# One stage of a 256-token block kernel: the two latent norms, the gate scalars and the bank copies behind the direct part are regrouped

## The chip, the core and the metric

One Trainium2 chip, one core. The metric is device microseconds (us) for one execution; lower is better. The kernel before takes 2758.27 us, the median of 3 runs (2757.26 to 2758.77). Its profile is one separate execution.

## The reference

Two transformer blocks run on 256 tokens of width 2048, in float32. The change lies in the first block's input part, which in the reference is:

```python
p = h @ w_in[l]                       # h: normed, modulated x, (256 x 2048)
c_q, c_kv, k_pe, q_g, k_g, v_g, z, b_logit, a_logit, gate_logits = _split_cols(p)
q  = _rmsnorm(c_q, q_norm) @ w_uq     # latents of 512 columns each
kv = _rmsnorm(c_kv, kv_norm) @ w_ukv
qkv = _causal_conv_silu(concat(q_g, k_g, v_g), conv_w)     # 4 taps, then silu
beta = jax.nn.sigmoid(b_logit)
g = -jnp.exp(A_log) * jax.nn.softplus(a_logit + dt_bias)
```

`beta` and `g` feed a chunked gated delta rule over 8 heads, and the normed latents feed 8-head causal attention. Later come the gates, `w_o`, the feed-forward part and the whole second block; the change does not touch those.

## The kernel before, in words

Data lies feature-major: a tile is 128 features by 256 tokens. Weights come from HBM in units of 512 KB, 8 tiles of 128x128 each. For each unit ScalarE rounds it (`hi`, L567, into one of 3 HI buffers) and VectorE subtracts (`lo`, L723, into LO), then TensorE multiplies both parts. A "wide" tile is a 512-column and a 256-column matmul (L361/L362 and L364/L365), a narrow one three of 256 columns (L367 to L369).

The first 16 column blocks of `w_in` are multiplied without that split (the direct part, L389): the 8 latent blocks, the block with `k_pe` and the two logit columns (`BA`), and 7 of the 24 q/k/v blocks. They fill all 8 PSUM banks, two blocks a bank. Their 16 banks' halves are then copied out, and 17 more `w_in` blocks follow as wide tiles, 16 tiles each. The change concerns what runs beside those tiles.

Every engine walks the same Python schedule (`walk`). `do(step, ...)` adds a step to its engine's program and gives a semaphore count to wait for. A side chain is a generator: `later(gen, lag, gap)` starts it `lag` tiles on and lets it make one step whenever `gap` tiles have passed. The list of chains is looked at after every second tile, so a gap of 3 is 4 tiles. `Ring.get` and `need` call `force`, which steps all chains with a gap of up to 3 whatever their due time. Each engine then executes its own program strictly in order. I count tiles from the first wide tile, t = 0.

Per unit, `feed` adds `hi` of a unit three ahead (it waits until TensorE is done with the unit whose buffer it takes) and one unit later its `lo`: `lo` of unit t/8 + 1 stands in VectorE's program at tile t, and TensorE needs it at tile t + 8.

The chains beside the wide tiles:
- `ev_c(j)`: copies latent block j out, squares it (L590), adds squares on GpSimd (`square_add`, L965), and for j = 3 and 7 goes on with `cnorm`: column sum by TensorE (`stat_sum`, L404), root (`root_guess` L603: Ln and Exp; `root_half`, `root_out`), then for each of 4 blocks a scaling (L769), `split_hi` (L578) and `split_lo` (L761) into H2. `finish_steps` of the second half calls `need(H2_tok, 3)`, which forces the chains until the first half is done.
- `ev_kpe`: copies BA and rotates `k_pe` (L422, L805 to L811, L426).
- `scalars`: transposes the logits (L431), `beta` (L613, Sigmoid), `softplus` (L617), then cumulative sums (L436, L437).
- `qkv_chain`: per q/k/v block a first tap on ScalarE (L649), three on VectorE (L817), tanh (L582), product (L769).
- `l2norm(0)`, `l2norm(1)` and `gdn()`, the delta rule, follow.

Of the kernel before, what the change touches and what calls it, by code (L numbers as in the profile page):

```python
# [17 lines left out]
TAPS = (5, 10)  # L18
# [151 lines left out]
def run(gen):  # L170
    for _ in gen:
        pass
# [30 lines left out]
def program(nc, xT, pos, cols_d, consts_d, wada, wst, bias_d, gain_d, out, log):  # L203
# [8 lines left out]
    with ctx:  # L212
# [74 lines left out]
        XSQ = B1[:, 0:16, :]  # L287
        R12, R1, ACC2 = B3[:, 0, :], B3[:, 1, :], B3[:, 2, :]
# [64 lines left out]
        def tensor(e):  # L353
# [190 lines left out]
            walk(dict(tile=tile, tile_tokens=tile_tokens, x_turn=x_turn, direct=direct, c_spread=c_spread, spin=spin, stat_add=stat_add, stat_sum=stat_sum, acc2_sum=acc2_sum, rope_turn=rope_turn, kpe_swap=kpe_swap, ba_turn=ba_turn,  # L544
# [5 lines left out]
        def scalar(e):  # L550
# [131 lines left out]
            def conv_tanh(y, t, ready, free):  # L682
# [4 lines left out]
                      gained=gained, square_sum=square_sum, root_table=root_table, root_guess=root_guess, sine=sine, beta=beta, softplus=softplus, gate_exp=gate_exp, row_square=row_square,  # L687
                      soft_exp=soft_exp, soft_scale=soft_scale, tap_first=tap_first, conv_first=conv_first, padded=padded, turned_rows=turned_rows, turned=turned, g_exp=g_exp, g_copy=g_copy, conv_square=conv_square, conv_affine=conv_affine, conv_tanh=conv_tanh))

        def vector(e):  # L690
# [144 lines left out]
            def cumulated(bk, summed, at):  # L835
# [4 lines left out]
                e.tensor_tensor(DK, GL, GC, sub).then_inc(S["l2_v"], 1)  # L840

# [104 lines left out]
            def conv_silu(t, y, grown):  # L946
# [7 lines left out]
                      ba_copy=ba_copy, softplus_in=softplus_in, decay_log=decay_log, cumulated=cumulated, beta_gate=beta_gate,  # L954
# [32 lines left out]
        def walk(mine, log=None):  # L987
# [386 lines left out]
            SQS = [Stats(x_stat), None]  # L1374

            def ev_c(j):
                def f(bk, tok, own):
                    cq_tok[j] = copy_out(CQ[j], bk, tok, own, x_used)
                    yield
                    while j > 3 and SQS[0].done is None:  # L1380
                        yield
                    if j == 4:
                        SQS[1] = Stats(*SQS[0].before, SQS[0].done)
                    SQS[j // 4].square(CQ[j], cq_tok[j])
                    if j % 4 == 3:
                        yield
                        yield from cnorm(j // 4)
                return f

            H2_tok = [None] * 16  # L1390

            def cnorm(half):
                k = yield from SQS[half].finish_steps(512, 1e-6, *([h_tok[15]] if half == 0 else [need(H2_tok, 3)]))
                name = "q_a_norm" if half == 0 else "kv_a_norm"
                for j in range(4):
                    i, t, fr = tv.get()
# [1185 lines left out]
```

## Time and profile before

| | |
|---|---|
| time, median of 3 runs | 2758.27 us |
| span of the profiled execution, first to last instruction | 2755.3 us |
| time of the profiled execution outside its span | not given on the page |
| TensorE busy | 2684.6 us, 97% |
| VectorE busy | 1931.7 us, 70% |
| ScalarE busy | 1315.8 us, 48% |
| GpSimd busy | 144.1 us, 5% |
| mean granted TensorE clock | 0.996 |

In the profile PE is TensorE, DVE is VectorE, ACT is ScalarE, POOL is GpSimd. Idle time stands in brackets with the instruction that ended it. An instruction's duration can overlap the start of the next; the distance from start to start is what a queue pays.

### The profile page before, as it was taken

Reading aid. Unit: us, or ns where it says so; the run is one execution under the profiler, and the core shown is the slowest. Engines: PE = TensorE matmul, PEld = TensorE weight load, DVE = VectorE, ACT = ScalarE, POOL = GpSimd, SP = SyncE. Lnnn points to the kernel's source line nnn. Section 1 sums busy time; section 2 is a strip of 40 time slices with the busy share of each in tenths; the row PEclk is TensorE's granted clock in tenths of the full one; section 3 lists DMA queues with packets and bytes.
Section 4 is the critical chain, followed back from the end, with each engine's and each line's share of the span. In section 5 each row is a group of like instructions: output and inputs, shape, how many; then the busy total and the mean of one; then the engine's idle time right before and its main releaser. Section 6 shows DMA issues by size and latency. Waiting matters only on the chain.

```text
span 2755.3 us, 41005 instructions
## 1 busy us (share of the span) xinstructions
PE 2684.6 (97%) x16144; PEld 2379.1 (86%) x16144; DVE 1931.7 (70%) x2983; ACT 1315.8 (48%) x2063; POOL 144.1 (5%) x132
## 2 busy tenths in 40 slices
PE   8989999999999999999999999999999999999998
PEld 7768988888899888888888889998888888888887
DVE  6868766876896886655555688997667466575665
ACT  2175644433544544444444454467555444444443
POOL 0000000000002000000000080111100000000000
PEclk9989999999999999999999999999999999999999
DMA  9944346666896786555555555554545555555554
GB/s 386 409 142 154 107 163 219 223 214 219 283 327 239 247 298 213 189 191 188 187 191 190 185 181 177 180 171 138 172 154 190 192 191 191 191 190 193 191 191 146
DMA packets 158737, 565.19 MB, mean 205 GB/s; under 512 B 17616, under 2 KB 21840, under 8 KB 158416
## 3 DMA queue, kind: packets, MB, share of 16 engines
q1 hardware_dynamic: 158544, 562.56, 59.8%
q8 instruction: 128, 2.10, 0.3%
q14 instruction: 65, 0.53, 0.1%
HBM read 560.39 MB, written 2.10 MB: 204 GB/s over the span
## 4 chain that ended last, share of the span: by engine, by line
PE 85%; DVE 8%; ACT 3%; DMA 2%; issue 1%; POOL 0%; DVEq 0%; ACTq 0%; SPq 0%; POOLq 0%
PE BK L364 17%; PE BK L362 17%; PE BK L365 9%; PE BK L361 8%; PE BK L376 4%; PE BK L377 4%; PE BK L378 4%; PE BK L367 4%; PE BK L369 4%; PE BK L368 4%; DVE LO L723 2%; PE BK L389 2%; PE BK L474 2%; DVE B L936 1%; ACT HI L567 1%
## 5 line engine op out<-in xcount | busy, mean ns | idle before, releaser
L567 ACT ACTIVATE HI<-RAW 128x1024 fp32r<-128x1024 f32 x824 | 873.6, 1060 | 1168.5 <-PE BK L362 638.6
L723 DVE TENSOR_TENSOR LO<-RAW,HI 128x1024 fp32r<-128x1024 f32 x824 | 1012.0, 1229 | 381.2 <-ACT HI L567 380.2
L364 PE MATMUL BK<-H,HI 128*128 128x512 f32 x2160 | 869.2, 405 | 17.3 <-DVE LO L723 16.7
L362 PE MATMUL BK<-H,HI 128*128 128x512 f32 x2128 | 840.8, 397 | 0.0
L365 PE MATMUL BK<-H,LO 128*128 128x256 f32 x2160 | 601.5, 278 | 0.0
L361 PE MATMUL BK<-H,LO 128*128 128x256 f32 x2128 | 595.8, 280 | 0.2 <-DVE H L761 0.2
L361 PEld LDWEIGHTS BK<-H,LO 128*128 128x128 f32 x2128 | 401.4, 189 | 93.7 <-DVE H L761 0.6
L365 PEld LDWEIGHTS BK<-H,LO 128*128 128x128 f32 x2160 | 408.2, 189 | 84.9 <-issue 1.0
L364 PEld LDWEIGHTS BK<-H,HI 128*128 128x128 f32 x2160 | 411.5, 190 | 29.7 <-DVE LO L723 20.5
L362 PEld LDWEIGHTS BK<-H,HI 128*128 128x128 f32 x2128 | 400.9, 188 | 3.9
L367 PE MATMUL BK<-H,HI 128*128 128x256 f32 x1280 | 376.2, 294 | 7.9 <-DVE LO L723 6.8
L369 PE MATMUL BK<-H,LO 128*128 128x256 f32 x1280 | 361.9, 283 | 0.0
L368 PE MATMUL BK<-H,HI 128*128 128x256 f32 x1280 | 361.8, 283 | 0.0
L367 PEld LDWEIGHTS BK<-H,HI 128*128 128x128 f32 x1280 | 244.8, 191 | 13.0 <-DVE LO L723 9.6
L368 PEld LDWEIGHTS BK<-H,HI 128*128 128x128 f32 x1280 | 244.9, 191 | 1.5
L369 PEld LDWEIGHTS BK<-H,LO 128*128 128x128 f32 x1280 | 244.6, 191 | 0.0
L376 PE MATMUL BK<-HI,H 128*128 128x512 f32 x512 | 199.2, 389 | 0.0
L378 PE MATMUL BK<-HI,H 128*128 128x512 f32 x512 | 199.2, 389 | 0.0
L377 PE MATMUL BK<-LO,H 128*128 128x512 f32 x512 | 199.2, 389 | 0.0
L761 DVE TENSOR_TENSOR H<-TV,H 128x256 fp32r<-128x256 f32 x116 | 49.2, 425 | 163.7 <-ACT H L578 163.6
L378 PEld LDWEIGHTS BK<-HI,H 128*128 128x128 f32 x512 | 96.1, 188 | 20.2
L377 PEld LDWEIGHTS BK<-LO,H 128*128 128x128 f32 x512 | 96.1, 188 | 19.9
(267 smaller groups left out, 2541.1 us busy)
## 6 DMA issues: line engine op xcount, KB each, us to landing
RAW<-wst_dram SPq DMA_DIRECT2D x837, 512.0 KB, 3.4
RAW<-wada_dram SPq DMA_DIRECT2D x155, 512.0 KB, 4.6
EARLY<-wada_dram SPq DMA_DIRECT2D x37, 512.0 KB, 11.0
EARLY<-wst_dram SPq DMA_DIRECT2D x19, 512.0 KB, 12.2
X<-xT_dram SPq DMA_DIRECT2D x8, 512.0 KB, 7.2
B<-bias_dram SPq DMA_DIRECT2D x32, 128.0 KB, 3.4
out_dram<-B SPq DMA_DIRECT2D x8, 256.0 KB, 2.2
B<-gain_dram SPq DMA_DIRECT2D x1, 1024.0 KB, 4.8
```

Of the source, the lines that this page charges most:

```text
L361: e.matmul(bk[:, 256:512], ll, H[:, k, 0:256], start=False, stop=False, skip_group_check=True)
L362: e.matmul(bk[:, :], hh, H[:, k, :], start=False, stop=last, skip_group_check=True).then_inc(S["tile"], 1)
L364: e.matmul(bk[:, :], hh, H[:, k, :], start=first, stop=False, skip_group_check=True)
L365: e.matmul(bk[:, 256:512], ll, H[:, k, 0:256], start=False, stop=last, skip_group_check=True).then_inc(S["tile"], 1)
L367: e.matmul(bk[:, 0:256], hh, H[:, k, 0:256], start=first, stop=False, skip_group_check=True)
L368: e.matmul(bk[:, 0:256], hh, H[:, k, 256:512], start=False, stop=False, skip_group_check=True)
L369: e.matmul(bk[:, 0:256], ll, H[:, k, 0:256], start=False, stop=last, skip_group_check=True).then_inc(S["tile"], 1)
L376: e.matmul(bks[m][:, :], H[:, k, 128 * m:128 * m + 128], hh, start=first, stop=False, skip_group_check=True)
L377: e.matmul(bks[m][:, :], H[:, k, 128 * m:128 * m + 128], ll, start=False, stop=False, skip_group_check=True)
L378: r = e.matmul(bks[m][:, :], H[:, k, 256 + 128 * m:384 + 128 * m], hh, start=False, stop=last, skip_group_check=True)
L567: e.activation(HI[:, u % NHL, :], raw_at(slot), ACT.Copy).then_inc(S["hi"], 1)
L723: e.tensor_tensor(LO[:, u % NHL, :], raw_at(slot), HI[:, u % NHL, :].bitcast(f32), sub).then_inc(S["lo"], 1)
```

## The change

Only the stage behind the direct part changes.
- The latents: after all 8 copies, two squares of 1024 columns on ScalarE, two adds on VectorE, one 512-column sum on TensorE, one root over 512 columns for both halves, 8 scalings in place, and per half one `hi` and one `lo` of 1024 columns. The GpSimd adds and the forcing `need` go.
- The scalars: `beta` is 1/(1 + exp(-x)) with Exp beside softplus's on ScalarE, and an add and a reciprocal on VectorE. No table is loaded for them.
- `qkv_chain` waits until root and soft gates are in the program, then takes three steps a block in place of two.
- Six of the seven q/k/v banks are copied by VectorE.
- Lags and gaps: `TAPS`, `LAT`. The last `w_in` block is narrow.

```diff
-TAPS = (5, 10)
+TAPS = (3, 7)
+LAT = (3, 0, 3, 12, 8, 24)
+        LSQ = B2[:, 0:8, :]
+        LSUM = SQ[:, 0:2, :].rearrange("p a t -> p (a t)")
+        LRS = RS[:, 0:2, :].rearrange("p a t -> p (a t)")
+            def latent_sum(bk, sums, consts, free):
+                q.wait_ge(sums, consts, free)
+                e.matmul(bk[:, :], cn("ones"), LSUM, start=True, stop=True).then_inc(S["st_p"], 1)
+            def latent_square(half, copied, free):
+                q.wait_ge(copied, free)
+                e.activation(LSQ[:, 4 * half:4 * half + 4, :], X[:, 4 * half:4 * half + 4, :], ACT.Square).then_inc(S["st_a"], 1)
+            def latent_hi(half, normed, free):
+                q.wait_ge(normed, free)
+                e.activation(H2[:, 4 * half:4 * half + 4, 0:256], X[:, 4 * half:4 * half + 4, :], ACT.Copy).then_inc(S["ev_a"], 1)
-            def beta(ready):
-                q.wait_ge(ready)
-                e.activation(m28(BETA), BA_T.rearrange("p (m h) -> p m h", m=2)[:, :, 0:8], ACT.Sigmoid).then_inc(S["l2_a"], 1)
-            def softplus(ready, at):
-                e.preload_act_table_set("natural_log_exp_and_others")
+            def soft_gates(ready, at):
                 q.wait_ge(ready)
                 e.activation(SPE, SPE, ACT.Exp, scale=-1.0).then_inc(S["l2_a"], 1)
+                e.activation(BETA, BETA, ACT.Exp).then_inc(S["l2_a"], 1)
+                e.activation(EA, col("A_log", 0, 8), ACT.Exp).then_inc(S["l2_a"], 1)
                 q.wait_ge(("l2_a", at + 1))
                 e.activation(SPE, SPE, ACT.Ln, bias=1.0).then_inc(S["l2_a"], 1)
-                e.activation(EA, col("A_log", 0, 8), ACT.Exp).then_inc(S["l2_a"], 1)
-            def softplus_in(ready, at):
+            def soft_in(ready, at):
                 q.wait_ge(ready)
...
+                e.tensor_scalar(m28(BETA), BA_T.rearrange("p (m h) -> p m h", m=2)[:, :, 0:8], -1.0, 80.0, mult, ALU.min).then_inc(S["l2_v"], 1)
...
+            def beta(grown, at):
+                q.wait_ge(grown)
+                e.tensor_scalar(BETA, BETA, 1.0, None, add).then_inc(S["l2_v"], 1)
+                q.wait_ge(("l2_v", at + 1))
+                e.reciprocal(BETA, BETA).then_inc(S["l2_v"], 1)
+            def bank_copy(dst, src, done, free):
+                q.wait_ge(done, free)
+                e.tensor_copy(dst, src).then_inc(S["ev_v"], 1)
+            def latent_pairs(squares):
+                q.wait_ge(squares)
+                rows = LSQ.rearrange("p (h r) t -> p h (r t)", h=2)
+                e.tensor_tensor(rows[:, :, 0:512], rows[:, :, 0:512], rows[:, :, 512:1024], add).then_inc(S["st_v"], 1)
+            def latent_total(pairs, free):
+                q.wait_ge(pairs, free)
+                rows = LSQ.rearrange("p (h r) t -> p h (r t)", h=2)
+                e.tensor_tensor(SQ[:, :, :], rows[:, :, 0:256], rows[:, :, 256:512], add).then_inc(S["st_v"], 1)
+            def latent_lo(half, rounded):
+                q.wait_ge(rounded)
+                e.tensor_tensor(H2[:, 4 * half:4 * half + 4, 256:512], X[:, 4 * half:4 * half + 4, :], H2[:, 4 * half:4 * half + 4, 0:256].bitcast(f32), sub).then_inc(S["ev_v"], 1)
             def ev_c(j):
                 def f(bk, tok, own):
                     cq_tok[j] = copy_out(CQ[j], bk, tok, own, x_used)
                     yield
-                    while j > 3 and SQS[0].done is None:
-                        yield
-                    if j == 4:
-                        SQS[1] = Stats(*SQS[0].before, SQS[0].done)
-                    SQS[j // 4].square(CQ[j], cq_tok[j])
-                    if j % 4 == 3:
-                        yield
-                        yield from cnorm(j // 4)
+            def latents():
+                for half in range(2):
+                    while cq_tok[4 * half + 3] is None:
+                        yield
+                    a = do("latent_square", "st_a", half, cq_tok[4 * half + 3], p1_end)
+                do("root_table", "st_a", n=0)
+                yield
+                v = do("latent_pairs", "st_v", a)
+                latent["sum"] = do("latent_total", "st_v", v, x_stat)
+                for _ in range(LAT[0]):
+                    yield
+                bi, bk, fr = mbank.get()
+                m = do("latent_sum", "st_p", bk, latent["sum"], tk_consts, fr)
+                yield
+                r = yield from rsqrt_steps(LRS, LSUM, bk[:, :], 1.0 / 512, 1e-6, m, h_tok[15], loaded=True)
+                latent["root"] = r
+                mbank.release(bi, r)
+                for half, name in ((0, "q_a_norm"), (1, "kv_a_norm")):
+                    for j in range(4):
+                        c = do("scaled", "ev_v", CQ[4 * half + j], CQ[4 * half + j], col(name, j), RS[:, half, :], mult, mult, r, a)
+                        if j % 2:
+                            yield
+                    h = do("latent_hi", "ev_a", half, c, raw_free[NRAW:])
+                    yield
+                    yield
+                    H2_tok[4 * half:4 * half + 4] = [do("latent_lo", "ev_v", half, h)] * 4
...
             def qkv_chain(ns):
+                while lin_tok["soft"] is None or latent["root"] is None:
+                    yield
...
                     v = do("taps", "ev_v", t, B1[:, j, :], COLS["conv_w"][0] + 4 * j, a, n=3)
+                    yield
                     s1 = do("tanh", "ev_a", B1[:, j, :], t, 1.0, v)
...
             def ev_first(n):
-                return ev_c(n) if n < 8 else ev_kpe if n == 8 else ev_qkv(n - 9, False)
+                return ev_c(n) if n < 8 else ev_kpe if n == 8 else ev_qkv(n - 9, None if FIRST.index(n) > 9 else False)
             for b, n in enumerate(FIRST):
                 own, bk, _ = held[b // 2]
                 later(ev_first(n)(bk[:, 256 * (b % 2):256 * (b % 2) + 256], done_tok[b | 1], (own, b % 2)))
-            later(scalars(), 16, 14)
+                if n == 8:
+                    later(latents(), 0, LAT[2])
+            later(scalars(), LAT[3], LAT[4])
             later(l2norm(0), 64, 6)
-            later(qkv_chain(Q03), 20, TAPS[0])
+            later(qkv_chain(Q03), LAT[5], TAPS[0])
             later(gdn(), 96, HAND)
             for n in REST:
-                run(block(H1, h_tok, 0, "w_in", 0, n, ev_qkv(n - 9, True), wide=True))
+                run(block(H1, h_tok, 0, "w_in", 0, n, ev_qkv(n - 9, n != REST[-1]), wide=n != REST[-1]))
```

The chain of `beta` in `scalars` follows `soft_gates` one step later; `Q47`, the second set of q/k/v blocks, runs with `TAPS[1]`.

## Rows read from the trace of the kernel before

**Rows 1.** The page: busy time by engine, and the granted TensorE clock in 40 slices.
```profile
PE 2684.6 (97%) x16144; PEld 2379.1 (86%) x16144; DVE 1931.7 (70%) x2983; ACT 1315.8 (48%) x2063; POOL 144.1 (5%) x132
...
PEclk9989999999999999999999999999999999999999
```
**Rows 2.** Windows behind the direct part: length, busy time by engine, clock, DMA share, GB/s.
```profile
143.90:161.20 17.30, 15.24 (x74) 12.74 (x74) 8.12 (x16) 12.04 (x32) 4.38 (x6) 0.90 0.42 152
161.20:167.40 6.20, 0.02 (x2) 0.01 (x1) 3.90 (x8) 4.97 (x8) 0.00 (x0) 0.77 0.00 0
167.40:175.05 7.65, 7.64 (x32) 6.37 (x32) 5.26 (x13) 7.50 (x12) 0.00 (x0) 0.74 0.40 137
175.05:179.24 4.19, 0.00 (x1) 0.01 (x1) 1.67 (x4) 4.16 (x7) 0.00 (x0) 0.87 0.00 0
186.00:200.00 14.00, 14.00 (x81) 12.23 (x81) 13.14 (x29) 7.53 (x16) 0.00 (x0) 1.00 0.53 169
```
**Rows 3.** Waits of that stretch: who waited for whom, us in total, times, longest.
```profile
PE BK L364 <- DVE LO L723: 10.4, 2, 6.2
...
PE BK L404 <- POOL SQ L965: 2.0, 1, 2.0
```
**Rows 4.** Timeline of PE: start, duration, instruction.
```profile
143.92 0.47 PE L364 MATMUL BK<-H,HI 128*128 128x512 f32 x1
...
171.39 0.39 PE L364 MATMUL BK<-H,HI 128*128 128x512 f32 x1
...
185.46 0.29 PE L436 MATMUL BK<-B,CN 128*128 128x16 f32 x2
...
186.13 0.28 PE L365 MATMUL BK<-H,LO 128*128 128x256 f32 x1
...
186.83 0.28 PE L365 MATMUL BK<-H,LO 128*128 128x256 f32 x1
```
**Rows 5.** Timeline of ACT.
```profile
150.51 1.28 ACT L601 ACT_TABLE_LOAD   x1
...
168.02 1.28 ACT L605 ACT_TABLE_LOAD   x1
169.31 0.47 ACT L605 ACTIVATE RS<-BK,CO 128x256 f32<-128x256 f32 x1
...
175.88 1.28 ACT L582 ACT_TABLE_LOAD   x1
```
**Rows 6.** Timeline of DVE.
```profile
140.78 3.70 DVE L723 TENSOR_TENSOR LO<-RAW,HI 128x1024 fp32r<-128x1024 f32 x3 [3.34 <-ACT HI L567]
...
164.68 1.52 DVE L817 SCALAR_TENSOR_TENSOR TV<-B,CO,TV 128x255 f32<-128x255 f32 x3 [1.40 <-ACT TV L649]
166.12 1.22 DVE L723 TENSOR_TENSOR LO<-RAW,HI 128x1024 fp32r<-128x1024 f32 x1
167.25 0.42 DVE L769 SCALAR_TENSOR_TENSOR B<-B,TV 128x256 f32<-128x256 f32 x1
```
**Rows 7.** Groups of the whole span by shape: count, busy us, mean ns, idle before.
```profile
L590 ACT ACTIVATE B<-X 128x1024 f32<-128x1024 f32 x4 | 4.2, 1056 | 3.3 <-DMA X<-xT_dram 3.3
...
L707 DVE COPY B<-BK 128x512 f32<-128x512 f32 x4 | 2.8, 692 | 5.0 <-PE BK L395 5.0
...
L899 DVE TENSOR_TENSOR X<-BK,X 128x512 f32<-128x512 f32 x4 | 2.8, 691 | 0.1
...
L944 DVE TENSOR_TENSOR B<-B 128x1024 f32<-128x1024 f32 x2 | 2.4, 1219 | 0.0
...
L769 DVE SCALAR_TENSOR_TENSOR TV<-X,CO,RS 128x256 f32<-128x256 f32 x8 | 3.8, 480 | 0.1
...
L769 DVE SCALAR_TENSOR_TENSOR X<-X,CO,B 128x256 f32<-128x256 f32 x16 | 11.5, 720 | 0.0
```
**Rows 8.** PE's waits from 200 to 500 us, then the window 250 to 475.
```profile
PE BK L468 <- DVE X L905: 1.9, 1, 1.9
...
250.00:475.00 225.00, 214.41 (x1455) 192.52 (x1454) 159.76 (x285) 113.57 (x244) 0.00 (x0) 1.00 0.47 158
```
**Rows 9.** By line: ns min/median/max, first and last start.
```profile
L486 PE MATMUL BK<-B,X x64: 272/272/373, 365.0 to 676.5; 64*128 64x128 f32 x64
...
L364 PE MATMUL BK<-H,HI x456: 389/397/988, 143.9 to 742.8; 128*128 128x512 f32 x152
```

More of the change, by code:

```diff
@@ L542, in conv_square_sum @@
                 r.then_inc(S["cv_p"], 1)
-            walk(dict(tile=tile, tile_tokens=tile_tokens, x_turn=x_turn, direct=direct, c_spread=c_spread, spin=spin, stat_add=stat_add, stat_sum=stat_sum, acc2_sum=acc2_sum, rope_turn=rope_turn, kpe_swap=kpe_swap, ba_turn=ba_turn,
+            walk(dict(tile=tile, tile_tokens=tile_tokens, x_turn=x_turn, direct=direct, c_spread=c_spread, spin=spin, stat_add=stat_add, latent_sum=latent_sum, stat_sum=stat_sum, acc2_sum=acc2_sum, rope_turn=rope_turn, kpe_swap=kpe_swap, ba_turn=ba_turn,
                       cumulate=cumulate, row_sum=row_sum, spread=spread, g_spread=g_spread, g_heads=g_heads, g_turn=g_turn,
@@ L953, in vector @@
                       stat_product=stat_product, total=total, gain=gain, normed=normed, rope_cos=rope_cos, rope_half=rope_half, rope_sin=rope_sin, taps=taps,
-                      ba_copy=ba_copy, softplus_in=softplus_in, decay_log=decay_log, cumulated=cumulated, beta_gate=beta_gate,
+                      ba_copy=ba_copy, soft_in=soft_in, beta=beta, decay_log=decay_log, bank_copy=bank_copy, latent_pairs=latent_pairs, latent_total=latent_total, latent_lo=latent_lo, cumulated=cumulated, beta_gate=beta_gate,
                       unit_rows=unit_rows, mla_mask=mla_mask, norm_column=norm_column, query_zero=query_zero, value_zero=value_zero, na_mask=na_mask, soft_max=soft_max, soft_share=soft_share,
@@ L1373, in walk @@
             cq_tok = [None] * 8
-            SQS = [Stats(x_stat), None]
+            H2_tok = [None] * 16
+            latent = {"sum": None, "root": None}
             def ev_c(j):
@@ L1379, in f @@
                     yield
-                    while j > 3 and SQS[0].done is None:
+                return f
+            def latents():
+                for half in range(2):
+                    while cq_tok[4 * half + 3] is None:
                         yield
-                    if j == 4:
-                        SQS[1] = Stats(*SQS[0].before, SQS[0].done)
-                    SQS[j // 4].square(CQ[j], cq_tok[j])
-                    if j % 4 == 3:
-                        yield
-                        yield from cnorm(j // 4)
@@ L1388, in ev_c @@
[L1388 to L1396, printed above, removed]
-                    c = do("scaled", "ev_v", t, CQ[4 * half + j], col(name, j), RS[:, 0, :], mult, mult, k, fr)
-                    yield
-                    H2_tok[4 * half + j] = yield from split(H2, 4 * half + j, t, c, raw_free[NRAW:])
-                    tv.release(i, H2_tok[4 * half + j])
+                    a = do("latent_square", "st_a", half, cq_tok[4 * half + 3], p1_end)
@@ L1414, in walk @@
             qkv_tok = [None] * 24
-            lin_tok = {"ba": None}
+            lin_tok = {"ba": None, "soft": None}
             raw_tok = [None] * 24
@@ L1420, in f @@
                 def f(bk, tok, own):
-                    if wide:
+                    if wide is None:
+                        raw_tok[j] = do("bank_copy", "ev_v", B1[:, j, :], bk, tok, x_stat)
+                        own[0].release(own[1], raw_tok[j])
+                        yield
+                    elif wide:
                         raw_tok[j] = yield from raw_sum(B1[:, j, :], bk, tok, own, x_stat)
@@ L1453, in scalars @@
                 mbank.release(bi, k)
-                a1 = do("beta", "l2_a", k)
-                k2 = do("softplus_in", "l2_v", k, n=2)
-                a2 = do("softplus", "l2_a", k2, n=3)
+                k2 = do("soft_in", "l2_v", k, n=3)
                 yield
+                a2 = do("soft_gates", "l2_a", k2, n=4)
+                lin_tok["soft"] = a2
+                yield
+                a1 = do("beta", "l2_v", (a2[0], a2[1] - 2), n=2)
                 g_tok = do("decay_log", "l2_v", a2, n=2)
@@ L1661, in walk @@
                 later(ev_first(n)(bk[:, 256 * (b % 2):256 * (b % 2) + 256], done_tok[b | 1], (own, b % 2)))
-            later(scalars(), 16, 14)
+                if n == 8:
+                    later(latents(), 0, LAT[2])
+            later(scalars(), LAT[3], LAT[4])
             later(l2norm(0), 64, 6)
-            later(qkv_chain(Q03), 20, TAPS[0])
+            later(qkv_chain(Q03), LAT[5], TAPS[0])
             later(gdn(), 96, HAND)
             for n in REST:
-                run(block(H1, h_tok, 0, "w_in", 0, n, ev_qkv(n - 9, True), wide=True))
-            while None in (cq_tok[7], RN["kpe"], lin_tok["ba"]):
+                run(block(H1, h_tok, 0, "w_in", 0, n, ev_qkv(n - 9, n != REST[-1]), wide=n != REST[-1]))
+            while None in (latent["root"], RN["kpe"], lin_tok["ba"]):
                 w.force()
-            c_used = [cq_tok[7], RN["kpe"], lin_tok["ba"], *p1_end]
+            c_used = [latent["sum"], RN["kpe"], lin_tok["ba"], *p1_end]
             pr = Ring(w, [B2[:, 11 + i, :] for i in range(4)], c_used)
@@ L1953, in walk @@
             x_tok = [None] * 16
-            ST = Stats(SQS[1].done, *x_free)
+            ST = Stats(latent["root"], *x_free)
             def ev_res(gate, ST, extra, wide):
```

2 lines of the change are left out of this document (1 added, 1 removed).

## The prediction

> **What bounds the kernel now.** I read the page first. TensorE is busy for 97% of the span and its clock stands at 9 tenths or more in 39 of 40 slices; only slice 3, which ends at 207 us, shows 8 [rows 1]. So a change to the other engines can only pay where TensorE stands still or runs slowly, and that is one place. The windows show it: TensorE does nothing from 161.2 to 167.4 and from 175.05 to 179.24 us, while from 186 us on it is busy for 14.00 of 14.00 us at full clock [rows 2]. The waits name the causes: two waits for LO, 10.4 us together, and one of 2.0 us for the GpSimd sums of squares [rows 3]. That is 12.4 us of standstill.
>
> The second cost is the clock. Full speed is 0.70 us for two wide tiles (186.13 to 186.83), or 0.3475 us a tile [rows 4]. After each of the three stops TensorE runs at 1.2 in place of 2.4 GHz: 150.84 to 154.4, 167.39 to 171.39 and 179.24 to about 185.0 us, 13.3 us in all, of which half, 6.7 us, is lost. The windows' 0.74 to 0.90 and the return of the 0.39 us matmul at 171.39 are its marks [rows 2, 4].
>
> Cross-check by position. L436 is issued at tile 58 and starts at 185.46 [rows 4]. Tile 96 is then reached at 185.82 + 38 x 0.3475 = 199.0 us. Without stops it would be 143.92 + 96 x 0.3475 + 2.2 us for the small f32 matmuls (rope 0.43, swap 0.43, sums 0.86, transposes and cumulation 0.47) = 179.5 us. The difference of 19.5 us agrees with 12.4 + 6.7, and is all that there is to gain.
>
> Why LO is late: it is not that VectorE is full (3.90 of 6.20 us in the long stop [rows 2]). Its queue holds the three taps ahead of LO (164.68, then 166.12 [rows 6]); they wait for a first tap on ScalarE, and that stands behind a chain of small H2 pieces passed to and fro, and table loads. Between 150.51 and 175.88 there are 8 loads [rows 5].
>
> **The change part by part.** Table loads: the root needs one, tanh one, and all roots and gates lie between them; 8 become 2, so ScalarE gets 6 x 1.28 = 7.7 us back [rows 5]. It is off the path itself; its worth is in the schedule below. (The Trainium skill, "ScalarE: Activation LUTs", section "What ACT_TABLE_LOAD costs", puts a drain of about 1.38 us on top of the 1.28, 2.66 together; the six would be worth 16.0 us of ScalarE. This trace disagrees: the load at 168.02 is followed by its Ln at 169.31, 1.29 us on [rows 5]. I take 1.28.)
>
> GpSimd's 6 adds and the 2.0 us wait for them go. The replacement is on VectorE: one add of 1024 columns, 1.22 us, one of 512, 0.69 us [rows 7]. The two squares are 1.06 us each, for 8 small ones of 0.32. The sum on TensorE is as wide as the two it replaces, so 0.
>
> Bank copies: 6 leave ScalarE (6 x 0.27 = 1.6 us) for VectorE, where they were not done before; the nearest row, 512 columns from PSUM at 0.69 us [rows 7], gives 0.33 us each from start to start, 2.0 us. They follow the three LO that end at 144.48 [rows 6], where VectorE is idle otherwise, so they cost nothing on the path.
>
> Root over 512 columns: 0.6 + 3 x 0.73 = 2.8 us in place of 2 x 1.75. Scalings: 8 as before. Bounds per scaling: 0.40 start to start (row of 0.48) and 0.72 (the row that is in place on X with its third operand in SBUF too) [rows 7]; I take 0.40, as operands and lines are those of the first and only the destination moves; the other end adds 8 x 0.32 = 2.6 us. Two wide lo: 1.14 each for 8 x 0.33. The new small gate steps on VectorE: 3 x about 0.2 us.
>
> Now the order. I lay the queues out, each instruction starting when its engine is free and what it waits for is done, with LO and wide lo 1.13, taps 1.44, product and bank sums 0.33 from start to start.
> - ScalarE: the 9 copies as before to 145.5, squares to 147.5, table 148.8, one bank copy 149.1.
> - VectorE: bank copies to 146.4, pairs at 147.6, total done 149.55, rope to 151.1, LO(35) 152.25.
> - TensorE reaches tile 12 at 148.5. The transpose takes the bank whose second half is that late bank copy, so it waits to 149.2: 0.7 us. At tile 16 the swap waits for rope: 0.35 us. Latent sum done and tile 16 at 152.5.
> - VectorE from there is never idle: gate inputs 152.85, LO(36) 154.0, root half and a bank sum 154.95, root 157.15, two scalings 157.95, taps 159.4, LO(37) 160.55, two scalings, gates and product 162.45, LO(38) 163.65, taps and bank sum 165.35, wide lo 166.5, two scalings 167.3, LO(39) 168.5, two scalings, product, cumulated 170.05, taps 171.5, LO(40) 172.6, bank sum, wide lo, product 174.6, LO(41) 175.7, then taps, product, sum 178.6.
> - TensorE: tile 24 at 155.3, 32 at 158.1, 40 at 160.85, 48 at 163.9 (0.1 wait for LO(38), cumulation), 56 would be 166.7 but gets LO(39) at 168.6, a stop of 1.9; 64 would be 171.4, gets LO(40) at 172.7, 1.3; 72 at 175.8 (0.3); from tile 80 no wait; tile 96 at 184.2.
>
> What is late next is thus again LO, now because VectorE's queue is truly full for 20 us, with stops of 1.9, 1.3 and three small ones, 4.7 us together. Sum: 199.0 - 184.2 = 14.8 us gained. The clock should hold: a stop of 1.9 us at L468 leaves the window's mean at 1.00 [rows 8], while one of 2.0 to L404 did not [rows 3, 4].
>
> Moved behind it: the first q/k/v set starts at tile 28 for 20 and keeps 12 tiles a block (three steps of 4 for two of 6), so `l2norm(0)` starts 12 tiles later; the second set takes 24 tiles a block for 20 and ends at tile 460 for 404. The delta rule then shifts 12 tiles, 4.2 us. Its last state matmul starts at 676.5, the wide tiles end after 742.8 [rows 9]: 66 us of cover, so 0. `l2norm(1)` moves 46 tiles, 16 us; its last rows end at 415 and the second head group begins after 486, so 0 too. But the neighbours in 250 to 475 us change, where TensorE stands for 225.0 - 214.4 = 10.6 us now [rows 8]. I see no sign; a third of it either way, 3.5 us, goes into the range. Weights are no limit: 512 KB a unit of 2.78 us is 188 GB/s, and DMA is idle in both long stops [rows 2]. The narrow last block costs as many columns, 0.
>
> The profile's span is 2755.3 us, 3.0 below the median of the runs; the page does not give what lies around it, and I subtract from the median. 2758.3 - 14.8 = 2743.5 us.
>
> **The rivals.**
> - A, no stops: if VectorE is quicker than laid out (ends overlap more), the whole 19.5 us comes, 2738.8. Against: it takes 4.7 of 20 full us.
> - B, the clock falls after the stop at tile 56. Price: two to four us at half speed, less the stop at tile 64 that it absorbs, at most 2 us, and with scalings at 0.72 another 2.6: 2748. For: 1.9 and 2.0 lie close.
> - C, the moved delta rule and taps collide with attention: all of the 10.6 us doubles and 14.8 shrinks to 4.2, 2754. For: VectorE is at 159.8 of 225 us there. Against: stops need alignment, and the taps get thinner.
> - D, slower: the same place, but its waits grow past the point where the clock falls. A stop of 2 us that takes the clock costs about 2 + 2 us [rows 3, 4]; it decides from four such stops beside 14.8 us, six for over 0.2%: 2766. Against: the longest there is 1.9 and the clock holds.
> - E, the regrouping moves nothing: if LO waited for its own HI and not for the queue. Then 2758. Against: in the long stop ScalarE is at 4.97 of 6.20 with loads and small pieces [rows 2].
>
> **How the numbers follow.** My forecast 0.74, A 0.08, B 0.08, C 0.05, D 0.03, E 0.02. Its own range: 14.8 with 3.5 either way and 2.6 for scalings, 2740 to 2750. I give 2738.5 to 2751, which takes in A and B. A measurement of this kernel tells about 0.2%, 5.5 us, from no change. Faster: forecast, A, B, and a fifth of C: 0.91; same: the rest of C and E, 0.06; slower: D, 0.03.
>
> **What would show it.** Right: two table loads from 147 to 177 us; no wait on GpSimd; TensorE's longest stop in 144 to 200 under 2.1 us and for LO; clock at 1.00; tile 96 at 184 us; busy in 250 to 475 within 3.5 us. Wrong: a stop over 3 us at tiles 48 to 72, a clock under 0.9 there, waits of the delta rule over 15 us, or taps that still stand ahead of LO waiting for ScalarE.

## The result, and the profile after

The changed kernel takes 2736.06 us (median of 4 runs, 2734.06 to 2737.55), the kernel before 2758.22 us (median of 4, 2757.26 to 2758.77). The ratio is 0.9919 (95% interval 0.9908 to 0.9931): 22.2 us faster. The forecast was 2743.5 us with a range of 2738.5 to 2751, so the direction was right and the gain was larger than the range allowed. The profiled execution took 2737.15 us, its span is 2735.0. One run of the kernel before (3297.52 us, beside e13) and one of e14 (3780.67 us) had a granted clock of 0.75 and 0.65 over the whole span; both are left out of every comparison.

The stretch behind the direct part first, then the place that matters later, as windows (length, busy time by engine, clock, DMA share, GB/s):

```profile
143.00:200.00 57.00, 54.06 (x300) 45.33 (x299) 53.69 (x103) 38.41 (x70) 0.00 (x0) 1.00 0.54 180
172.00:184.00 12.00, 12.00 (x66) 10.09 (x67) 11.79 (x22) 6.28 (x12) 0.00 (x0) 1.00 0.58 181
234.00:451.00 217.00, 212.37 (x1466) 194.01 (x1465) 161.10 (x291) 116.34 (x248) 0.00 (x0) 1.00 0.49 165
340.00:420.00 80.00, 78.92 (x496) 69.47 (x496) 64.86 (x111) 38.43 (x72) 0.00 (x0) 1.00 0.61 206
```

Before, the same stretch had 12.4 us of standstill and three spells at half clock [rows 2, 3]. Now TensorE stands for 2.9 of 57 us and the clock's mean is 1.00. VectorE is busy for 53.7 of the 57: it is the engine that is full now. The waits of that stretch (who waited for whom, us in total, times, longest):

```profile
PE BK L368 <- DVE LO L735: 2.1, 2, 1.1
PE BK L439 <- ACT B L579: 0.5, 1, 0.5
PE BK L434 <- DVE B L813: 0.2, 1, 0.2
```

They answer to [rows 3]: no wait on GpSimd, and of the 10.4 us for LO 2.1 are left. In the timeline of TensorE the two stops stand at tiles 56 and 64:

```profile
148.82 0.44 PE L439 MATMUL BK<-CN,B 128*128 128x128 f32 x2 [0.54 <-ACT B L579]
...
167.89 0.50 PE L368 MATMUL BK<-H,HI 128*128 128x512 f32 x1 [1.13 <-DVE LO L735]
...
171.96 0.50 PE L368 MATMUL BK<-H,HI 128*128 128x512 f32 x1 [0.99 <-DVE LO L735]
```

ScalarE's timeline has two table loads where [rows 5] began a series of eight. The root needs the first, tanh the second, and the roots and small gates lie between them:

```profile
147.09 1.28 ACT L617 ACT_TABLE_LOAD   x1
...
159.13 1.28 ACT L590 ACT_TABLE_LOAD   x1
```

And VectorE's, which answers to [rows 6]: the bank copies follow the early LO, and behind the root every instruction follows the one before it, without a gap that the timeline would mark.

```profile
143.89 2.07 DVE L863 COPY B<-BK 128x256 f32<-128x256 f32 x6
147.10 1.23 DVE L868 TENSOR_TENSOR B<-B 128x1024 f32<-128x1024 f32 x1 [1.15 <-ACT B L602]
148.37 0.69 DVE L873 TENSOR_TENSOR SQ<-B 128x512 f32<-128x512 f32 x1
...
156.69 0.88 DVE L781 SCALAR_TENSOR_TENSOR X<-X,CO,RS 128x256 f32<-128x256 f32 x2
157.50 1.51 DVE L829 SCALAR_TENSOR_TENSOR TV<-B,CO,TV 128x255 f32<-128x255 f32 x3
158.93 1.22 DVE L735 TENSOR_TENSOR LO<-RAW,HI 128x1024 fp32r<-128x1024 f32 x1
```

Where in the span did the gain come? LO instructions come in the same order in both kernels, 824 of them, so the start of the n-th LO of this form in one trace can be set against that in the other. The difference (before minus after) is 15.9 us at the 13th (196.9 and 181.0), 16.9 at the 49th (339.1 and 322.2), 21.9 at the 53rd (363.5 and 341.6), between 21 and 27 from there to 430 us, and 20.4 at the 201st (920.5 and 900.1). LO is made ahead of its use, so single values move by some microseconds. There are two places. One is the stretch that was forecast. The other lies between 340 and 420 us, where the kernel before stood still for 5.0 us and the changed kernel, with 78.92 of 80.00, hardly does. Over about the same work, 250 to 475 us before [rows 8] and 234 to 451 us now, the standstill went from 10.6 to 4.6 us.

### The profile page after: what moved, and what is told of

Read it like the earlier page. It is cut to its first block, busy times and chain, and to the rows that moved or that the text cites. A ratio compares the mean times of both kernels' runs of the same rounds, so it can differ in the third digit from the quotient of the medians.

```text
span 2735.0 us, 40983 instructions
## 1 busy us (share of the span) xinstructions
PE 2677.6 (98%) x16158; PEld 2376.9 (87%) x16158; DVE 1929.8 (71%) x2983; ACT 1304.3 (48%) x2037; POOL 139.0 (5%) x126
## 4 chain that ended last, share of the span: by engine, by line
PE 87%; DVE 7%; DMA 3%; ACT 2%; issue 1%; DVEq 0%; ACTq 0%; SPq 0%
PE BK L368 17%; PE BK L366 17%; PE BK L369 9%; PE BK L365 8%; PE BK L371 4%; PE BK L373 4%; PE BK L372 4%; PE BK L380 4%; PE BK L381 4%; PE BK L382 4%; PE BK L393 2%; DVE LO L735 2%; PE BK L482 2%; DMA RAW<-wst_dram 1%; DVE B L973 1%
## 5 line engine op out<-in xcount | busy, mean ns | idle before, releaser
L371 PE MATMUL BK<-H,HI 128*128 128x256 f32 x1296 | 381.4, 294 | 8.8 <-DVE LO L735 8.5
L372 PE MATMUL BK<-H,HI 128*128 128x256 f32 x1296 | 367.5, 284 | 0.0
L382 PEld LDWEIGHTS BK<-HI,H 128*128 128x128 f32 x512 | 96.1, 188 | 20.1
L380 PEld LDWEIGHTS BK<-HI,H 128*128 128x128 f32 x512 | 96.1, 188 | 19.8
```

What stands on the lines that cost most here:

```text
L371: e.matmul(bk[:, 0:256], hh, H[:, k, 0:256], start=first, stop=False, skip_group_check=True)
L372: e.matmul(bk[:, 0:256], hh, H[:, k, 256:512], start=False, stop=False, skip_group_check=True)
L380: e.matmul(bks[m][:, :], H[:, k, 128 * m:128 * m + 128], hh, start=first, stop=False, skip_group_check=True)
L382: r = e.matmul(bks[m][:, :], H[:, k, 256 + 128 * m:384 + 128 * m], hh, start=False, stop=last, skip_group_check=True)
```

## The experiments

Gains are against runs of the kernel before on the same chip. The changed kernel's own is 22.2 us, and the intervals are 2.3 to 3.7 us either way. Windows, timelines and LO starts come from one profiled execution of each kernel.

**e1: the changed kernel with the second q/k/v set paced as before.**

```diff
-TAPS = (3, 7)
+TAPS = (3, 10)
 (qkv_chain, behind the taps)
-                    yield
+                    if ns is Q03:
+                        yield
```

> The changed kernel, but the second set of q/k/v blocks runs as before: tanh stands right behind its taps in ScalarE's program, two steps of 10 tiles a block. Theory P (pace: the gain of about 5 us in 250 to 475 us comes from tanh no longer standing in front of hi while the taps run, and from the thinner second set): 2736 + 4 to 6 = 2740 to 2742 us; ScalarE's wait for the taps from tile 280 on rises from 3 to about 15 us. Rival S (shift: it comes from the delta rule starting 12 tiles later against attention): unchanged within 1.5 us, 2735 to 2737.5.

Measured: 2742.2 us (2740.65 to 2744.97), ratio 0.9946 (0.9933 to 0.996), gain 15.8. About 6 us of the gain are gone, and one stop, with the slow clock behind it, holds them. TensorE's timeline:

```profile
264.36 0.36 PE L371 MATMUL BK<-H,HI 128*128 128x256 f32 x1 [4.35 <-DVE LO L735]
```

VectorE's, before it:

```profile
258.01 0.68 DVE L932 TENSOR_TENSOR B<-B,CN 128x512 f32<-128x512 f32 x1
258.80 0.69 DVE L936 TENSOR_TENSOR X<-BK,B 128x512 f32<-128x512 f32 x1
...
260.98 0.69 DVE L942 TENSOR_TENSOR X<-CN,X 128x512 f32<-128x512 f32 x1
261.59 1.51 DVE L829 SCALAR_TENSOR_TENSOR TV<-B,CO,TV 128x255 f32<-128x255 f32 x3
```

And ScalarE's:

```profile
263.13 0.42 ACT L590 ACTIVATE B<-TV 128x256 f32<-128x256 f32 x1 [4.84 <-DVE TV L829]
...
263.85 0.36 ACT L579 ACTIVATE B<-BK 128x256 f32<-128x256 f32 x1
```

Read them as one chain. The delta rule's token tile begins with five wide instructions on VectorE, each waiting for the one before it, 3.6 us in all. I call these five instructions the burst below. The taps are queued behind the burst, the tanh waits for the taps on ScalarE for 4.84 us, and the copy of a bank (L579) stands behind the tanh. TensorE stops at tile 280. The matmul there waits for a ScalarE step and for LO, and two events come 0.02 us apart: the bank copy ends at 264.22 and an LO at 264.24. The view names LO, as the later one. But that is the 37th LO. The changed kernel has done tiles 280 to 283 by 259.3, before its own 37th LO starts (260.52), so tile 280 needs no more than the 36th, which had ended at 258.1 in e1. The wait was for the bank copy. VectorE is busy for 5.72 of the 6 us from 258 to 264, ScalarE for 1.16: two chains met on VectorE. The clock then fell as well (0.54 from 264.7 to 268.0).

**e2: before, with only the new pace of the second set.** Of the change, this is the part that looks like housekeeping.

```diff
-TAPS = (5, 10)
+TAPS = (5, 7)
 (qkv_chain, behind the taps)
+                    if ns is Q47:
+                        yield
```

> The kernel before with one edit: in the second set of q/k/v blocks a step lies between taps and tanh, three steps of 8 tiles a block. Theory P: 4 to 6 us faster, 2752 to 2754 us, with VectorE and ScalarE unchanged up to tile 164. Rival S: 2757 to 2759.

Measured: 2751.18 us (2749.42 to 2755.81), ratio 0.9979 (0.997 to 0.9987), gain 6.8. The stretch of the forecast is as before; TensorE is busy for 219.78 us from 250 to 475, before 214.41 [rows 8]. So part of the gain has nothing to do with the latents' roots, the tables or the taps behind the direct part.

**e3: the changed kernel with sigmoid and softplus back on their own tables.**

```diff
+            def beta_gate_old(ready):
+                e.activation(..., ACT.Sigmoid)
             def soft_gates(ready, at):
+                e.preload_act_table_set("natural_log_exp_and_others")
                 e.activation(SPE, SPE, ACT.Exp, scale=-1.0)
-                e.activation(BETA, BETA, ACT.Exp)
...
```

> The changed kernel with the gates computed as before, by Sigmoid and with the table preload, in the same steps. Theory Q (VectorE's queue is full from 151 to 180 us, so each us that its taps wait is a us of TensorE): two loads more, 2.6 us of ScalarE at tile 28, first taps at about 160 in place of 157.5, time 2 to 3 us longer, 2738 to 2739.5; the stop at tile 56 near 2.5 us and perhaps the clock falls, then up to 2741. Rival R (the loads are hidden, the wide latents did it all): 2736 within 1 us.

Measured: 2738.53 us (2737.37 to 2740.03), ratio 0.9931 (0.9919 to 0.9944), gain 19.5. The two tables more and what they delay are worth 2.7 us, which lies within the intervals; the 13th LO is 3.2 us later in this trace than in the changed kernel's. ScalarE's timeline:

```profile
157.12 1.28 ACT L631 ACT_TABLE_LOAD   x1
158.42 0.22 ACT L631 ACTIVATE B<-B 128x16 f32<-128x16 f32 x1
158.65 1.28 ACT L634 ACT_TABLE_LOAD   x1
...
161.88 1.28 ACT L590 ACT_TABLE_LOAD   x1
```

and TensorE's:

```profile
163.66 0.50 PE L368 MATMUL BK<-H,HI 128*128 128x512 f32 x1 [2.13 <-DVE LO L739]
```

The first taps come 3.8 us later than in the changed kernel (160.42 for 156.65), and LO behind them makes a stop of 2.13 us.

**e4: the changed kernel, but the q/k/v taps start early and wait for nothing.**

```diff
-LAT = (3, 0, 3, 12, 8, 24)
+LAT = (3, 0, 3, 12, 8, 20)
 (qkv_chain)
-                while lin_tok["soft"] is None or latent["root"] is None:
-                    yield
```

> The changed kernel, but the first set starts at tile 20 and does not wait for root and gates. Theory Q: tanh's table at tile 24, then the logarithm's and tanh's again, two to three loads more, in front of them hi of tile 32; 1 to 4 us longer, 2737 to 2740. Rival R: the taps fill VectorE's queue two steps earlier and nothing else changes: 2735 to 2737.

Measured: 2751.29 us (2750.01 to 2753.32), ratio 0.9977 (0.9968 to 0.9986), gain 6.7. That is 15.5 us lost, far more than I expected. Its window:

```profile
143.00:200.00 57.00, 49.12 (x259) 40.28 (x258) 51.44 (x101) 40.98 (x72) 0.00 (x0) 0.97 0.46 157
```

The longest wait in it:

```profile
PE BK L434 <- DVE B L813: 4.0, 1, 4.0
```

There are six table loads again (147.35 to 164.53), since tanh now comes between root and gates. The 4.0 us is one that I had not thought of: rope's first operation on VectorE is queued behind the taps, these wait for ScalarE, and the kpe swap on TensorE waits for rope; the clock then fell to 0.57 from 157 to 160 us. By the n-th LO the loss is 7.6 us at the 13th, 9.2 at the 21st and 15.5 after 900 us. About half of the loss stands in the stretch and half behind it. There it is spread over several stops. After two of them, 2.15 us at 585.12 and 2.79 us at 683.93, the clock fell too (0.50 from 586.3 to 589.6 and from 685.3 to 688.6). What starts them was not traced.

**e5: all bank copies on ScalarE.** **e9: hi and lo of the latents in pieces of 256 columns.** Both on the changed kernel.

```diff
 (e5)
-ev_qkv(n - 9, None if FIRST.index(n) > 9 else False)
+ev_qkv(n - 9, False)
 (e9)
-                    h = do("latent_hi", ...)
+                    hs = [do("split_hi", ...) for j in range(4)]
-                    H2_tok[...] = [do("latent_lo", ...)] * 4
+                    H2_tok[...] = [do("split_lo", ...) for j in range(4)]
```

> The changed kernel with all bank copies on ScalarE. ScalarE is 1.6 us later with hi of tile 24 and 32, which have slack there, VectorE idles for 2.0 us more before the latents' adds; the transpose at tile 12 waits for the same copy. 2736 within 1 us; if ScalarE's late hi reaches LO(35), up to 2738.

> The changed kernel, but hi and lo of the normed latents in four pieces of 256 columns each, issued together, in place of one of 1024. Theory N (width as such is worth little when the pieces stand together): VectorE 2 x (4 x 0.33 - 1.13) = 0.4 us more in its full stretch, ScalarE 2 x (4 x 0.32 - 1.0) = 0.6; 2736 to 2737.5 us. Rival W (width matters): over 2738.

Measured: e5 2737.62 us (2735.74 to 2739.44), ratio 0.9923 (0.9909 to 0.9936), gain 20.6; e9 2737.93 us (2734.31 to 2738.53), ratio 0.9923 (0.9909 to 0.9936), gain 20.7. Both differ from the changed kernel by some 1.5 us, which these runs cannot tell from nothing. The width of the latents' hi and lo and the second copying engine are not where the gain is. The wide squares, root and sums stay in both.

**e6 and e7: which half of the new pace matters, on the changed kernel.**

```diff
 (e6: more taps per tile, but with the extra step)
-TAPS = (3, 7)
+TAPS = (3, 5)
 (e7: the pace of the change, but without the step)
-TAPS = (3, 7)
+TAPS = (3, 11)
-                    yield
+                    if ns is Q03:
+                        yield
```

> The changed kernel, the second q/k/v set with the step between taps and tanh kept, but denser: three steps of 6 tiles, 18 tiles a block for 24 (before: 20). Theory P1 (it is the step: tanh no longer stands in ScalarE's queue in front of hi while taps wait in VectorE's): 2736 to 2738 us. Theory P2 (it is the thinner load of VectorE): denser than before, so 2742 to 2744, like the run with the old second set.

> The changed kernel, the second set thin but without the step: two steps of 12 tiles, 24 tiles a block, tanh right behind its taps. P1: 2740 to 2743 us, ScalarE's wait for taps near 15 us. P2: 2736 to 2738.

Measured: e6 2736.21 us (2734.63 to 2738.39), e7 2736.22 us (2734.09 to 2738.43), ratio 0.9918 for both (0.9905 to 0.9932, 0.9904 to 0.9931). Neither half is needed by itself: the theories "a thinner pace" and "the extra step" both fall as general causes. In both, taps end before the burst (at 257.3 before 258.7 us in e6, at 256.8 before 257.8 in e7), the tanh follows them at once, and the stop of e1 is gone. e6 says one thing more: with 18 tiles a block the second set ends early, and the root of `l2norm(1)` (373.3 us) falls behind the same LO as in the kernel before, the 57th, 8 us ahead of the next token tile's burst (381.3 us). Time and standstill are those of the changed kernel all the same (79.19 of 80.00 us busy from 340 to 420). So where the delta rule starts 12 tiles later, the later `l2norm(1)` is not needed.

**e8: before, with only the order: q/k/v taps wait for the gates and for the latents' rows.** The formulas, the GpSimd sums and the small pieces stay; the order by itself takes three of the eight table loads away (five from 151.12 to 179.28).

```diff
             def qkv_chain(ns):
+                while lin_tok["soft"] is None or H2_tok[7] is None:
+                    yield
...
```

> The kernel before, where the first set of q/k/v blocks waits until gates and both latent norms stand in the program; nothing wide, no new formula, squares and adds as before. Theory O (order: no tanh table between the roots, no taps in front of LO while ScalarE works through roots): the two LO waits of 10.4 us and their slow clock nearly go, the GpSimd wait stays; 11 to 14 us faster, 2744 to 2747. Rival W (the wide operations are what shortens it): 2752 to 2757.

Measured: 2747.63 us (2746.99 to 2748.11), ratio 0.9959 (0.9946 to 0.9971), gain 10.6. By the 13th LO it has gained 10.5 of the changed kernel's 15.9 us. Its waits from 143 to 200 us:

```profile
PE BK L364 <- DVE LO L723: 3.5, 1, 3.5
PE BK L404 <- POOL SQ L965: 2.2, 2, 2.1
```

So order alone gives two thirds of the forecast place, a little under the 11 to 14 us that I expected; the GpSimd wait and one stop for LO are what the rest of the change removes. How that rest divides between wide squares, wide root and the adds on VectorE no run shows.

**e10: the changed kernel, with the latents' scalings and their hi and lo 34 turns later.** They are needed only from tile 272, and stand in the stretch where VectorE is full.

```diff
                 mbank.release(bi, r)
+                for _ in range(34):
+                    yield
```

> The changed kernel, the scalings, hi and lo of both halves 136 tiles later (tile 164 to 200), after the first q/k/v set. It takes 8 x 0.40 + 2 x 1.13 = 5.5 us out of VectorE's full stretch from 157 to 174 us. Theory Q (VectorE's full queue makes the last stops): the stops for LO at tiles 56, 64 and 72, 2.4 us together, go, and 2733 to 2734.5 us are left. Rival: the stops move to tile 200 and it stays at 2736.

Measured: 2732.64 us (2730.33 to 2735.17), ratio 0.9907 (0.9894 to 0.9921), gain 25.9. This is the lowest time of all; it was not measured side by side with the changed kernel, and the two intervals of the ratio overlap. Its window:

```profile
143.00:200.00 57.00, 56.17 (x318) 48.15 (x318) 51.63 (x98) 38.45 (x70) 0.00 (x0) 1.00 0.57 192
```

The two stops for LO are gone; only the 0.5 and 0.2 us waits are left. The 13th LO starts at 176.9, 4.1 us before that of the changed kernel.

**e11, e12: before, with the second set's pace in two other forms.**

```diff
 (e11)
-TAPS = (5, 10)
+TAPS = (5, 5)
+                    if ns is Q47:
+                        yield
 (e12)
-TAPS = (5, 10)
+TAPS = (5, 11)
```

> The kernel before, second set with a step between taps and tanh, 18 tiles a block (before: 20, no step). P1 (the step): 2751 to 2753 us. P2 (thinner): 2757 to 2760. P3 (where taps and tanh fall against the delta rule's runs of wide VectorE instructions; any other beat helps): 2751 to 2754.

> The kernel before, second set in two steps of 12 tiles, 24 tiles a block, tanh right behind its taps. P1: 2756 to 2759 us. P2 and P3: 2751 to 2754.

Measured: e11 2757.93 us (2755.79 to 2759.75), ratio 0.9997 (0.9988 to 1.0006), no gain; e12 2752.05 us (2749.26 to 2754.7), ratio 0.9977 (0.9968 to 0.9986), gain 6.5. In e11 the stop of the kernel before is still there, in e12 it is not:

```profile
395.18 0.76 PE L468 MATMUL BK<-CN,X 128*128 128x128 f32 x4 [1.90 <-DVE X L905]
```

On the kernel before the number of tiles over which the second set is spread decides. It sets where that set ends, and so where `l2norm(1)` starts. In e12 and e2 its root stands at 401 us, behind the burst (387.8 and 387.6); in e11 at 388.3, ahead of it (391.5).

**e13 and e14: one chain of the meeting is moved and nothing else.** In the kernel before, the timelines at that place read, TensorE's first:

```profile
397.73 0.66 PE L468 MATMUL BK<-CN,X 128*128 128x128 f32 x4 [1.90 <-DVE X L905]
```

VectorE's, the root and then the burst:

```profile
391.34 0.42 DVE L773 TENSOR_SCALAR RS<-BK 128x256 f32<-128x256 f32 x1 [0.23 <-ACT RS L605]
...
394.02 0.69 DVE L895 TENSOR_TENSOR B<-B,CN 128x512 f32<-128x512 f32 x1
...
396.99 0.69 DVE L905 TENSOR_TENSOR X<-CN,X 128x512 f32<-128x512 f32 x1
```

ScalarE's table loads:

```profile
389.54 1.28 ACT L601 ACT_TABLE_LOAD   x1
...
392.30 1.28 ACT L582 ACT_TABLE_LOAD   x1
```

The root of `l2norm(1)`, with its two table loads and its operations on VectorE, falls on the burst of the delta rule's second token tile.

```diff
 (e13)
-            later(l2norm(1), 0, 6)
+            later(l2norm(1), 48, 6)
 (e14: l2norm(0), and with it the delta rule, 12 tiles later)
+                if hg == 0:
+                    yield
+                    yield
```

> The kernel before, l2norm(1) due 48 tiles later (tile 432), second q/k/v set untouched. Theory L (what costs 5 to 6 us in 340 to 420 us is that l2norm(1), its root with two table loads and its row scalings, falls on the start of the delta rule's second token tile; a thinner second set only helps by moving it): 2751 to 2754 us. Rival T (the thinner load of taps itself): 2757 to 2759.

> The kernel before, l2norm(0) and with it the delta rule 12 tiles later, as the changed kernel has it, nothing else; l2norm(1) stays at tile 384. Theory L: the two no longer meet, or less: 2752 to 2755 us. Rival T: 2757 to 2759, or slower by a new meeting with the taps near 260 us, as in the run with the old second set.

Measured: e13 2752.54 us (2750.44 to 2755.04), ratio 0.998 (0.9971 to 0.9989), gain 5.8; e14 2755.54 us (2752.69 to 2756.28), ratio 0.9985 (0.9976 to 0.9995), gain 2.8. Windows of 340 to 420 us and the slices that differ, in the kernel before:

```profile
340.00:420.00 80.00, 75.04 (x477) 65.58 (x476) 55.78 (x101) 38.49 (x80) 0.00 (x0) 1.00 0.49 165
...
350.00:360.00 10.00, 8.49 (x56) 7.16 (x55) 4.49 (x11) 5.81 (x16) 0.00 (x0) 1.00 0.33 109
...
390.00:400.00 10.00, 8.11 (x47) 6.80 (x46) 9.46 (x17) 6.10 (x9) 0.00 (x0) 1.00 0.40 132
400.00:410.00 10.00, 8.76 (x57) 7.53 (x56) 10.00 (x19) 3.98 (x7) 0.00 (x0) 1.00 0.72 262
```

The same window of e13:

```profile
340.00:420.00 80.00, 79.30 (x510) 69.79 (x510) 59.80 (x102) 41.57 (x86) 0.00 (x0) 1.00 0.57 187
```

And of e14:

```profile
340.00:420.00 80.00, 79.19 (x514) 70.65 (x515) 58.99 (x109) 40.91 (x89) 0.00 (x0) 1.00 0.48 158
```

Moving either chain empties the place: 5.0 us of standstill become 0.7 and 0.8. e13 keeps that gain: 4.3 of its 5.8 us are this window (79.30 for 75.04). Its profiled execution was its slowest run, 2755.04 us. There it is 6.0 us ahead up to 700 us by the n-th LO and 2.6 behind 945 us; the median of its eleven runs keeps 5.8. e14 pays most of it elsewhere: the delayed first token tile puts its burst (271.84 to 275.5) on VectorE ahead of the bank sum that TensorE needs at tile 280. The tanh (270.47) had passed before, so it has no part in this stop: what stood behind the burst on VectorE went first, and the stop ends 0.15 us after the bank sum. TensorE's timeline, then VectorE's:

```profile
277.45 0.55 PE L367 MATMUL BK<-H,HI 128*128 128x256 f32 x1 [5.16 <-DVE B L727]
```

```profile
276.89 0.41 DVE L727 TENSOR_TENSOR B<-BK,TE 128x256 f32<-128x256 f32 x1
```

The trace of e13 also tells what the 1.90 us of the kernel before are made of. Its timeline of TensorE at that place:

```profile
381.86 1.02 PE L451 MATMUL BK<-X,CN 128*128 128x512 f32 x2
...
389.19 0.59 PE L441 MATMUL BK<-TE,CN 128*128 128x256 f32 x2
...
391.22 0.66 PE L468 MATMUL BK<-CN,X 128*128 128x128 f32 x4
```

L441 is a row sum of `l2norm(1)`; three of them (384.13, 386.66, 389.19) now stand between the delta rule's L451 and L468, where the kernel before had none. With them TensorE comes to L468 9.4 us behind L451 and does not wait. Before, it came there 8.1 us behind L451 (387.71 to 395.83) and stood still. So 1.2 of the 1.90 us are work that TensorE could have done there and had done earlier. The other 0.7 are the burst: it ends 10.0 us behind L451 before and 9.3 in e13, because the exponential that it needs (L668) waited on ScalarE behind the root's first table load and its two operations (391.66, where L891 ended at 390.78; in e13 384.95 and 384.92).

## Why the prediction was wrong

**What bounds the kernel: right.** The stretch behind the direct part, its two kinds of loss and their cause (LO behind taps that wait for ScalarE) were as read. e8 and e4 show the order from both sides, by the 13th LO: the order alone gives 10.5 of the 15.9 us, and without it the rest of the change has 8.3. The two add up to more than the whole, so they are not separate shares. That e4 as a whole is left with 6.7 us is not this stretch alone, since half of its loss comes behind 200 us.

**The laid-out queue: right, 1.1 us short.** I forecast tile 96 at 184.2, 14.8 us gained. Tile 64 starts at 171.96, and from 172 on TensorE has no gap, so tile 96 is at 171.96 + 32 x 0.3475 = 183.1: 15.9 us, as the 13th LO says. 0.5 us of it is that the stretch begins earlier in this execution. The stops stood at the tiles named, 56 and 64, and waited for LO as named; I had 1.9 and 1.3 us, measured were 1.13 and 0.99. The waits for the late bank copy and for rope's half, 0.7 and 0.35, measured 0.54 and 0.15.

**The single costs: right.** Bank copies 0.33 us each start to start (2.07 for six). Scalings at the low bound: a pair lasts 0.88 and the next instruction starts 0.81 behind it, as in 156.69 to 157.50. Wide lo 1.22 with a pitch of 1.13; pairs 1.23, total 0.69. Table loads 1.28 each, two for eight.

**The clock should hold at a stop of 1.9 us: held, but not tested**, the stops being shorter, and the ground for it was weak. It was one trace. In e11 the same stop of 1.90 us at L468 took the clock (last section).

**"The delta rule then shifts 12 tiles ... so 0" and "`l2norm(1)` moves 46 tiles ... so 0 too": this is the step that failed.** For both chains I asked whether their results still arrive in time, which they do, and for neither what it stood on before. They stood on each other: the root of `l2norm(1)` at 390.8, the burst of the second token tile at 394.0. Either shift parts them. Moving `l2norm(1)` alone is worth 5.8 us (e13), its pace alone 6.8 and 6.5 (e2, e12), and a pace that leaves it in place 0 (e11). Moving the delta rule alone empties the same window (79.19 for 75.04) but meets another wait at 272 us and keeps 2.8 (e14). The changed kernel moves both, so its gain there belongs to neither alone. With the delta rule moved, `l2norm(1)` can stay where it was (e6, gain 22.0), as long as the pace keeps the taps from standing between burst and tanh (e1, 6 us lost). With the 15.9 of the first place, e13's 5.8 make 21.7, and 22.2 were measured.

The next sentence of the prediction had the place and its full size, 10.6 us of standstill from 250 to 475 [rows 8], and then took "no sign; a third of it either way". Measured were 219.89 us busy there for 214.41, 5.5 us of the 10.6, or 6.0 over the same work. The third was a guess without a row; the trace had the rows for more, since the 1.90 us wait of [rows 8] was quoted for the clock and not asked what it was.

**The rivals.** A (no stops, 2738.8) has nearly the number, but for another reason: there were stops, and only e10 takes them away. B, C and D did not occur. Waits that take the clock, as D has them, show in e4; a meeting of delta rule and taps, as C has it, costs e1 its 6 us. D's price was summed wrongly: six stops of 4 us less 14.8 give 2767.5, not 2766. E is out: its two waits for LO fell from 10.4 to 2.1 us.

**Open.** Of the 5.0 us of standstill in 340 to 420, 1.5 stand at 354 to 356 in attention's transposes (L500). They vanish in e13. The squares (L632, 356.01) and row sums (L441, 356.10 and 358.63) of `l2norm(1)` stand there in the kernel before and not in e13, and the copy (L664) that one of the stops waits for starts at 355.35 and at 352.00 us; why it comes later was not traced. The 0.88 us at 408.99 wait for a copy behind an HI that had itself waited 4.83 us for its weights. e8 is ahead by 14.8 us at the 122nd LO (659 us) and by 9.2 from the 146th (746 us) on; where these 5.6 us go is not known, nor why the changed kernel falls from 24.4 to 20.4 between 766 and 945 us. Profiled, it stops once for 3.51 us at 749.22 with HI waiting 7.08 us for weights, and runs at 0.50 clock behind it; its runs lie in two pairs, near 2734.5 and 2737.3, and whether this stop is what parts them was not tested.

## What to carry to other kernels

When a side chain moves, list what it stands beside before and after, not only when its result is due: a burst of dependent wide instructions (3.6 us here) delays what is queued behind it on its engine, and through that the queues of the others (e1: VectorE, then ScalarE, then TensorE). Where TensorE must wait for such a burst, other work of its own can stand in the wait (the row sums of e13). A long wait in the trace of before is a place where a shift can win, so give it a price, even if the change is not aimed at it. Here filler work was best behind the roots and gates whose table it would break up (e4, e8), and work that was due much later best outside the stretch where its engine is full (e10, whose interval still overlaps the changed kernel's). When a view names one releaser for a wait on several, look for the other (e1).

## What the runs showed of the hardware

The length of a stop does not by itself say whether the clock falls, at least up to 2.4 us. The clearest case is one stop in many traces. The wait of L404 for the GpSimd sums lasts 2.03 to 2.05 us in the kernel before and in e2, e8, e11, e12, e13 and e14. Behind it the clock fell in the kernel before, e12 and e13, and held in e2, e8, e11 and e14. The kernel before, then e2:

```profile
150.84:154.00 3.16, 3.16 (x10) 2.69 (x11) 1.02 (x1) 2.18 (x5) 0.89 (x2) 0.51 0.36 115
```

```profile
149.95:153.00 3.05, 3.05 (x18) 2.68 (x19) 0.99 (x1) 2.45 (x6) 1.17 (x2) 1.00 0.34 103
```

The same for the stop of 1.90 us at L468, in the kernel before and in e11:

```profile
397.80:401.00 3.20, 3.20 (x20) 2.88 (x21) 3.13 (x7) 0.56 (x2) 0.00 (x0) 1.00 0.02 6
```

```profile
395.90:398.90 3.00, 3.00 (x11) 2.52 (x10) 2.97 (x6) 0.72 (x2) 0.00 (x0) 0.50 0.15 26
```

And e3 kept its clock behind 2.13 us, as the changed kernel did behind 2.43 us at 889.33 (1.00 to 892):

```profile
163.60:168.00 4.40, 4.34 (x26) 3.85 (x27) 4.29 (x12) 3.04 (x6) 0.00 (x0) 1.00 0.54 174
```

Of the longer stops, those looked at lost it: 3.51 us (0.50 behind it), 3.97 (0.80, then 0.57), 4.35 (0.54), 5.16 (0.50 from 277.45 to 281). Several short ones can do it too: in e8 TensorE was busy for 2.67 of the 4 us from 280 to 284, with no stop over 0.65 us, and ran at 0.50 from 284.2 to 287.4. The two levels are the 2.4 and 1.2 GHz of the prediction.

In the traces here a table load costs ScalarE its 1.28 us and no more, also when two come close together: in e3 the load of 157.12 is followed by its activation at 158.42, 1.30 us on, and the next load starts at 158.65. The Trainium skill's "ScalarE: Activation LUTs", section "What ACT_TABLE_LOAD costs", has a drain of about 1.38 us besides; no load looked at here shows one.
